# Turns of the normalised input, one weight unit and two layer-norm tasks placed at other steps of a hand-ordered two-block kernel

## The reference

```python
for l in range(DEPTH_2):
    shift, scale, gate = ...            # from c_act @ ada_w[l] + ada_b[l]
    h = rms_norm_2(x, norm_g[l]) * (1.0 + scale) + shift
    z = h @ w_in[l]
    q_lat, kv_lat, k_rope, mla_gate, conv_in, conv_gate = jnp.split(z, splits, axis=-1)
    ...                                 # attention over q, k, v gives mla_out
    u_val, u_gate = jnp.split(conv_in + glu_b[l], 2, axis=-1)
    u = causal_depthwise_conv(u_val * jax.nn.sigmoid(u_gate), dw_w[l], dw_b[l])
    u = jax.nn.silu(layer_norm(u, conv_ln_g[l], conv_ln_b[l]))
    u = u @ w_pw[l] + b_pw[l]
    conv_out = u * jax.nn.silu(conv_gate)
    y = jnp.concatenate([mla_out, conv_out], axis=-1) @ w_out[l]
    x = x + gate * y
```

## Time and profile before

| | |
|---|---|
| median of 3 runs | 1953.4 us |
| profiled execution | 1953.4 us, span 1951.6 us |
| PE busy | 1932.6 us (99%) |
| DVE busy | 1504.0 us (77%) |
| ACT busy | 1014.2 us (52%) |
| POOL busy | 125.4 us (6%) |
| granted TensorE clock over the span | 0.999 |

### The profile page before, as it was taken

One profiled execution on the slowest core, in us unless ns is written; L12 is line 12 of the kernel. 1 busy time (PEld: TensorE's weight loads), 2 busy tenths in 40 slices (PEclk: granted clock), 3 DMA queues, 4 the chain that ended last, 5 costly groups with the idle time before them and its releaser, 6 DMA issues.

```text
span 1951.6 us, 24848 instructions
## 1 busy us (share of the span) xinstructions
PE 1932.6 (99%) x9262; PEld 1618.0 (83%) x9262; DVE 1504.0 (77%) x2044; ACT 1014.2 (52%) x1477; POOL 125.4 (6%) x88
## 2 busy tenths in 40 slices
PE   9999999999999999999999999999999999999999
PEld 7888888888888888888888888888887888888877
DVE  5786777777677777777776568888898688888986
ACT  5545455445535444444435455566646455666553
POOL 1221233000000000000000000001100000010000
PEclk9999999999999999999999999999999999999999
DMA  7787867789888888988887646655565465555554
GB/s 254 240 270 236 284 223 249 255 278 309 277 304 278 286 302 276 302 293 293 292 282 252 194 155 175 186 166 158 155 205 181 144 190 164 177 165 156 195 181 142
DMA packets 225947, 445.10 MB, mean 228 GB/s; under 512 B 15795, under 2 KB 57189, under 8 KB 225571
## 3 DMA queue, kind: packets, MB, share of 16 engines
q1 hardware_dynamic: 225443, 443.08, 70.0%
q10 hardware_dynamic: 384, 0.44, 0.1%
HBM read 441.34 MB, written 2.11 MB: 227 GB/s over the span
## 4 chain that ended last, share of the span: by engine, by line
PE 81%; DVE 10%; ACT 4%; POOL 3%; issue 2%; DMA 0%; ACTq 0%; DVEq 0%; POOLq 0%
PE P L704 25%; PE P L706 25%; PE P L705 24%; DVE WL L1062 3%; PE P L467 2%; DVE CA L1059 2%; POOL ST L1464 1%; ACT WH L1033 1%; PE P L499 1%; DVE FB L1359 1%; POOL QK L1490 1%; PE P L576 1%; DVE X L1423 1%; PE P L586 1%; PE P L587 1%
## 5 line engine op out<-in xcount | busy, mean ns | idle before, releaser
L1062 DVE TENSOR_TENSOR WL<-RAW,WH 128x1024 fp32r<-128x1024 f32 x648 | 790.2, 1224 | 310.4 <-ACT WH L1033 309.3
L1033 ACT ACTIVATE WH<-RAW 128x1024 fp32r<-128x1024 f32 x648 | 670.5, 1045 | 565.1 <-PE P L706 434.6
L704 PE MATMUL P<-WH,AH 128*128 128x512 f32 (+1 forms) x1536 | 604.7, 394 | 4.5 <-DVE WL L1062 2.8
L706 PE MATMUL P<-WH,AL 128*128 128x512 f32 (+1 forms) x1536 | 594.7, 387 | 0.0
L705 PE MATMUL P<-WL,AH 128*128 128x512 f32 (+1 forms) x1536 | 593.4, 386 | 0.0
L704 PE MATMUL P<-WH,BH 128*128 128x512 f32 x896 | 353.0, 394 | 0.0
L706 PE MATMUL P<-WH,BL 128*128 128x512 f32 x896 | 349.2, 390 | 0.0
L705 PE MATMUL P<-WL,BH 128*128 128x512 f32 x896 | 348.6, 389 | 0.0
L704 PEld LDWEIGHTS P<-WH,AH 128*128 128x128 f32 x1536 | 288.9, 188 | 61.7 <-issue 4.0
L706 PEld LDWEIGHTS P<-WH,AL 128*128 128x128 f32 x1536 | 288.7, 188 | 59.1
L705 PEld LDWEIGHTS P<-WL,AH 128*128 128x128 f32 x1536 | 289.1, 188 | 54.6
(11 more groups left out here) (249 smaller groups left out, 1392.1 us busy)
## 6 DMA issues: line engine op xcount, KB each, us to landing
RAW<-in_ada_w_dram SPq DMA_DIRECT2D x192, 512.0 KB, 5.0
RAW<-in_mlp_w_in_dram SPq DMA_DIRECT2D x128, 512.0 KB, 4.7
RAW<-in_mlp_w_out_dram SPq DMA_DIRECT2D x128, 512.0 KB, 5.2
RAW<-in_sb_w_qkv_dram SPq DMA_DIRECT2D x96, 512.0 KB, 5.0
RAW<-in_w_in_dram SPq DMA_DIRECT2D x80, 512.0 KB, 4.1
RAW<-in_w_in_dram SPq DMA_DIRECT2D x128, 256.0 KB, 3.1
RAW<-in_w_out_dram SPq DMA_DIRECT2D x64, 512.0 KB, 3.8
RAW<-in_sb_w_o_dram SPq DMA_DIRECT2D x32, 512.0 KB, 5.4
```

What stands on the lines that cost most here:

```text
L704: e.matmul(o, xh, wh, start=u.first and k == 0, stop=False)
L706: return e.matmul(o, xl, wh, start=False, stop=u.last and k == u.nk - 1)
L1033: e.activation(WH[:, n % NH, 0:size], RAW[:, i % NR, 0:size], ACT.Copy).then_inc(w_high, 1)
L1062: return e.tensor_tensor(o, x, h.bitcast(F32), ALU.subtract)
```

## The change

In `chain`, unit b+4 is no longer held back: its weights are converted at step b (the default) and not at step b+1. The turn (0, 3) moves from behind unit b+1 to the three turns ahead of unit b. `h_shift(l, 0, 3)` moves from step b+2, where it stood ahead of `h_split(l, 1, 2)`, to step b+3. In the layer norm, `ln_rstd` moves from the front of step s+5 to the end of step s+6, and `gate_act` from step s+6 to `zend - 1 + 9`; `zend` is b+92, so that is b+100, which is s+2, behind `ln_centre`.

```diff
         def chain(g, l, b):
             by_row.extend((b - 2, b))
-            held.update({b + 2: b - 1, b + 3: b, b + 4: b + 1})
+            held[b + 2], held[b + 3] = b - 1, b
...
-            after[b - 1] += [("h_turn", l, 0, q) for q in range(3)]
+            after[b - 1] += [("h_turn", l, 0, q) for q in range(4)]
...
             after[b] += [("h_split", l, 1, 1)]
-            after[b + 1] += [("h_shift", l, 0, 2), ("h_split", l, 0, 2), ("h_turn", l, 0, 3)]
-            after[b + 2] += [("h_turn", l, 1, 2), ("h_shift", l, 0, 3), ("h_split", l, 1, 2)]
-            after[b + 3] += [("h_split", l, 0, 3), ("h_turn", l, 1, 3), ("h_split", l, 1, 3)]
+            after[b + 1] += [("h_shift", l, 0, 2), ("h_split", l, 0, 2)]
+            after[b + 2] += [("h_turn", l, 1, 2), ("h_split", l, 1, 2)]
+            after[b + 3] += [("h_shift", l, 0, 3), ("h_split", l, 0, 3), ("h_turn", l, 1, 3), ("h_split", l, 1, 3)]
...
-            after[s + 5].insert(0, ("ln_rstd", l))
+            after[s + 6].append(("ln_rstd", l))
...
-            after[s + 6].append(("gate_act", l))
+            s = zend[l] - 1
+            after[s + 9].append(("gate_act", l))
```

## The result

The changed kernel takes 1968.08 us in the median of six runs (1966.7 to 1969.94), the kernel before 1953.63 beside it (1953.12 to 1954.12). The ratio is 1.0075 with a 95% interval of 1.0061 to 1.0087: slower by 14.5 us. Forecast were 1966.2 us and a range of 1961.3 to 1969.3. The profiled execution took 1966.83 us with a span of 1965.0.

The account below looks back on a forecast made before the run. TensorE, busy 99% of the span, was taken to bound the kernel. 2 x (3.0 start of a layer + 1.9 layer norm + 1.5 clock) = 12.8 us on 1953.4 gave 1966.2 us, range 1961.3 to 1969.3.

Parts of the forecast that it names:

- The fourth turn: Start of a layer, ahead of unit b: what follows comes 0 to 0.47 us later, taken as 0.1; no later gain.
- Unit b+4 one step earlier: Start of a layer: shift (0,2) ends later behind the early weights, so the turn (1,2) is 0.4 us late.
- The bank of the turn (1,3): Start of a layer: TensorE stops 3.5 us for the bank of (0,3), drained later; 3.0 us a layer (2.8 to 3.4).
- gate_act: Layer norm: table load and silu delay VectorE's conversions from unit s+6 by 1.36 us; TensorE begins s+6 1.3 us late.
- The drain: Layer norm, rival: the table switch has a drain the rows don't show, 1.4 us a layer, 1969.0 us; chance 0.03.
- ln_rstd: Layer norm: GpSimd takes 0.70 us, VectorE multiplies 1.9 us late, and TensorE stands 1.15 us for the result.
- the layer norm: Both moves there together: the end is set by the low parts ULL, 1.9 us a layer, at most 2.45.
- The clock: Behind each layer's 3.5 us stop the granted clock falls, costing 1.5 us (0 to 3); rival, clock holds: 0.27.

Follow-up runs that it names:

- hold5_turn: Kernel before with the turn (0,3) ahead of unit b and the weights of unit b+5 held back to step b+2: 1952.59 us, ratio 0.9993.
- hold5_only: Kernel before with only the weights of unit b+5 held back to step b+2: 1952.69 us, ratio 0.9992.
- after: The changed kernel, with all edits of the change to the kernel before: 1968.08 us, ratio 1.0075.
- after_shift_back: Changed kernel with h_shift(0,3) put back at step b+2, ahead of h_split(1,2): 1958.85 us, ratio 1.0027.
- bank_only: Kernel before with only the turn (0,3) moved ahead of unit b and h_shift(0,3) moved to step b+3: 1963.05 us, ratio 1.0051.
- ln_rstd_s4: Kernel before with ln_rstd moved to the end of step s+4: 1953.48 us, ratio 0.9999.
- add_between: Kernel of after_shift_back with the addition o_add of chunk 2 moved from step s+5 to s+6, right behind ln_rstd: 1956.84 us, ratio 1.0014.
- gate_act_only: Kernel before with only gate_act moved, to step s+2 behind ln_centre: 1956.8 us, ratio 1.0018.
- late_add: Kernel before with o_add of chunk 3 moved from step s+9 to the front of step s+11: 1958.46 us, ratio 1.0024.

## Why the prediction was right, point by point

*The fourth turn.* I took 0.1 us, it was 0.0: the turn (1,0) came 5.13 us after the first in both kernels. It gained nothing later either, as foreseen (hold5_turn against hold5_only).

*Unit b+4 one step earlier.* The turn (1,2) did wait for the shift, in after and after_shift_back, 0.2 us idle; it came 0.3 us later than before where 0.4 was foreseen, and that cost nothing in the end. The 0.1 us gain that I mentioned and left out is real and nearer to 0.2.

*The bank of the turn (1,3).* The large term was right in mechanism and size. 3.0 us a layer were forecast and 2.99 measured in layer 0, where the clock held. The idle time shown is 3.24 us and not the 3.5 of the forecast, but the starts of the turns (1,2) and (1,3) lie 1171.66 - 1164.52 = 7.14 us apart where they lay 3.63 apart before, which is 3.5 more. bank_only shows that its two edits suffice, after_shift_back that without the later shift the whole cost is gone.

*gate_act.* Forecast were a delay of 1.36 us and 1.3 us of stop; measured are 1.34 us of VectorE's wait, 1.36 of TensorE's stop and +1.42 for the norm where it stood alone. The drain that the Trainium skill ("ScalarE: Activation LUTs", section "What ACT_TABLE_LOAD costs") adds to a load didn't appear: the load follows the square by 0.01 us and takes 1.28.

*ln_rstd.* This is the mis-sized term. The step took GpSimd's power at 0.70 us from the earlier trace rows, and the layer norm at 1.9 us a layer. The power took 1.61 us, and the norm 2.89 in layer 0, above even the 2.45 that I gave as the term's upper bound; VectorE's L1387 came 2.88 us later relative to the squares, not 1.9. The missing 0.91 us of the power account for nearly all of the 1.0. The row that I used was the right instruction with another neighbour: before, VectorE ran FB <- P, G beside it, one operand of which is in PSUM, and in the new place WL <- RAW, WH, both in SBUF. VectorE in the kernel before, beside the earlier trace rows:

```profile
1869.17 0.67 DVE L1418 TENSOR_TENSOR FB<-P,G 128x512 f32<-128x512 f32 x1
```

ln_rstd_s4 made it slow in a fast kernel by that neighbour, and add_between made it fast again in a slow one. This is what the Trainium skill says in "SBUF — State Buffer", section "Who interferes with whom": an instruction of VectorE with two inputs in SBUF contends with one of GpSimd that reads SBUF, through the read interface that both share. The trace agrees: 1.61 against 0.70. In ln_rstd_s4 the power ended 0.56 us behind the conversion (1868.21 + 1.61 against 1868.05 + 1.21). Had I weighed the page, I would have looked for a longer time; it gives no size for so small an instruction.

The trace of before had a size. The same power on 128x2, elsewhere in layer 0, with six short instructions of VectorE beside most of it that read SBUF alone (the first is shown), took 1.22 us:

```profile
1247.36 1.22 POOL L1464 TENSOR_TENSOR ST<-ST,CST 128x2 f32<-128x2 f32 x1 [16.57 <-DVE ST L1270]
```
```profile
1247.26 0.22 DVE L1249 TENSOR_TENSOR RK<-KR,TK 128x64 f32<-128x64 f32 x1
```

So it isn't the conversion alone that slows it. The order of start may matter too: at 34.16 us of the same trace the power took 0.70, though a conversion began 0.50 us behind it. That is one case. Besides its operands the conversion is also longer and wider than the addition (1.21 us and 1024 columns against 0.68 and 512), and no run parts how much of the 0.91 us comes from that.

*The clock.* I took one fall of 1.5 us behind each long stop and none behind the stops of about 1.2 us. In the profiled execution there was one behind the long stop of layer 1 (+1.5) and none behind that of layer 0, but one behind the stops of 1.36 and 1.99 us in layer 1's norm (+1.1), and none behind those of 1.36 and 1.96 us in layer 0's. The sum, 2.6 against 3.0, is right, the assignment isn't. In gate_act_only the clock fell behind a stop of 1.36 us in layer 1 and not in layer 0. So whether it falls there is not settled by the length of the stop. Nor is a stop needed. In three of the twelve profiled executions (gate_act_only, late_add, hold5_only) the clock also fell near 337 us, in code that no edit touches, where TensorE had been busy for 3.91 of the 4 us before, part of it with sixteen matmuls of one column (L499); in the other nine it stayed at 1.00 there. In gate_act_only:

```profile
332.00:336.00 4.00, 3.91 (x34) 3.72 (x34) 3.35 (x7) 2.04 (x5) 1.44 (x3) 1.00 0.80 261
336.00:340.00 4.00, 4.00 (x12) 3.09 (x12) 3.43 (x3) 0.82 (x1) 2.35 (x2) 0.57 0.62 207
```

The stop of 1.99 us at the start of the kernel, on which I built the price, was followed by a fall in the kernel before and by none in the changed one. What else decides was not tried. The clock spreads the times: the six runs of the changed kernel lie 3.2 us apart and those of the kernel before 1.0.

In all: 2 x (3.0 + 2.9) = 11.8 us of waits and 2.6 of clock make 14.4 behind the first turn of layer 0; the medians differ by 14.5. This near agreement is in part luck, as the 2.6 is of one execution, 1.3 us faster than the median. The same holds for the forecast: the layer norm was put 2.0 us too low over both layers, and the result lies within the range because the range was wide, not because it foresaw a slow power.

## What to carry to other kernels

Where buffers are taken strictly in turn, moving a producer forward moves the release that a later one depends on: write down the order of takes, and for each the task that drains the one four before, and where that task stands in its engine's queue. A duration is a row together with its neighbours; before a small GpSimd instruction is moved, look at what VectorE will run beside it. And price a stop of TensorE with its clock: here the start's stops of 3.2 to 4 us cost nothing more, about 1.5 or about 2.5 us, and stops of 1.4 to 2.3 us from nothing to 1.5 (late_add). Where a later wait is there to shrink, the lost clock can cost nothing (after_shift_back).

## What the hardware showed that I had not expected

In the layer norm of all twelve traces, both layers, GpSimd's power on 128x2 took 0.70 us beside the VectorE addition with one PSUM operand (16 times) and 1.61 us beside the conversion with two SBUF operands (8 times), within 0.01. The granted clock fell to 0.50 behind stops of 1.36 us (gate_act_only) and 1.99 us (after) in one layer and stayed at 1.00 behind the same stop of the other layer, and behind a stop of 3.24 us in layer 0 of the changed kernel. It also fell, in three of twelve executions, behind sixteen matmuls of one column and no stop over 0.1 us.
